# Two small buffers are declared ahead of the weight slots of a two-block transformer kernel

## The reference

```python
# first block:  x = x + fox_mixer(rmsnorm(x));  x = x + nsa_mixer(rmsnorm(x));  x = rmsnorm(x)
# second block: x = x + hgrn2(rmsnorm(x)); x = x + conv_ffn(rmsnorm(x))
#               x = x + mla(rmsnorm(x));   x = x + conv_ffn(rmsnorm(x))
proj = h @ w_in                       # 1024 x 4112 (fox), 1024 x 3632 (nsa), 1024 x 4096 (hgrn2), 1024 x 576 (mla)
y = (attention_or_recurrence(proj) * gate) @ w_out      # 1024 x 1024 in each mixer
u = h @ w_up                          # 1024 x 5632, twice
y = (silu(conv(gate)) * conv(up)) @ w_down              # 2816 x 1024, twice
```

## Time and profile before

| | |
|---|---|
| three runs | 1018.06, 1018.89, 1016.15 us |
| profiled execution | 1013.38 us |
| its span | 1011.6 us |
| granted TensorE clock, mean | 0.994 |
| PE (matmul) busy | 983.1 us, 97% |
| PEld (weight load) busy | 934.2 us, 92% |
| DVE busy | 766.2 us, 76% |
| ACT busy | 549.7 us, 54% |

### The profile page before, as it was taken

The page is one execution under the profiler, slowest core; times in us unless marked ns, Lnnn a source line. Parts: engine busy times, 40 slices in busy tenths (PEclk is TensorE's granted clock), DMA queues, the critical chain, the costliest instruction groups (busy, mean ns, idle before and its releaser), DMA issues. The chain is left out here.

```text
span 1011.6 us, 20271 instructions
## 1 busy us (share of the span) xinstructions
PE 983.1 (97%) x8132; PEld 934.2 (92%) x8132; DVE 766.2 (76%) x1300; ACT 549.7 (54%) x869; POOL 66.7 (7%) x54
## 2 busy tenths in 40 slices
PE   7999999999999999999999999999999999999997
PEld 5999999898788999899999999999997899999997
DVE  5765776867887768498667888888867668878785
ACT  5644555365666656643556554555775565544541
POOL 3100004000000410000030000000001410000000
PEclk9999999999999999999999999999999999999999
DMA  9544345793212556500564767675531456666631
GB/s 283 175 126 132 135 144 148 222 307 97 84 43 85 161 172 194 182 1 1 162 173 142 213 185 207 172 221 149 152 125 43 126 166 193 184 204 170 201 130 42
DMA packets 184141, 153.08 MB, mean 151 GB/s; under 512 B 12477, under 2 KB 176900, under 8 KB 184068
## 3 DMA queue, kind: packets, MB, share of 16 engines
q1 hardware_dynamic: 183858, 152.01, 50.4%
q10 hardware_dynamic: 210, 0.05, 0.0%
HBM read 148.91 MB, written 1.05 MB: 148 GB/s over the span
## 5 line engine op out<-in xcount | busy, mean ns | idle before, releaser
L447 PE MATMUL bank<-h_high,w_high 128*128 128x256 f32 x1312 | 372.6, 284 | 4.6 <-DVE work L1943 1.4
L448 PE MATMUL bank<-h_low,w_high 128*128 128x256 f32 x1312 | 365.5, 279 | 0.0
L449 PE MATMUL bank<-h_high,w_low 128*128 128x256 f32 x1312 | 365.4, 279 | 0.0
L399 ACT ACTIVATE w_high<-ring 128x2048 fp32r<-128x2048 f32 x137 | 261.7, 1913 | 136.2 <-PE bank L449 129.7
L409 DVE TENSOR_TENSOR w_low<-ring,w_high 128x2048 fp32r<-128x2048 f32 x118 | 270.3, 2292 | 27.1 <-ACT w_high L399 26.8
L447 PEld LDWEIGHTS bank<-h_high,w_high 128*128 128x128 f32 x1312 | 248.7, 190 | 6.8 <-issue 5.5
L448 PEld LDWEIGHTS bank<-h_low,w_high 128*128 128x128 f32 x1312 | 247.3, 188 | 0.5 <-issue 0.5
L449 PEld LDWEIGHTS bank<-h_high,w_low 128*128 128x128 f32 x1312 | 247.3, 188 | 0.0
L447 PE MATMUL bank<-ffn_hidden_high,w_high 128*128 (+1 forms) x352 | 98.3, 279 | 2.8 <-DVE ffn_hidden_low L1128 2.8
L448 PE MATMUL bank<-ffn_hidden_low,w_high 128*128 (+1 forms) x352 | 98.1, 279 | 0.0
L449 PE MATMUL bank<-ffn_hidden_high,w_low 128*128 (+1 forms) x352 | 98.1, 279 | 0.0
(11 more groups left out here) (352 smaller groups left out, 1730.7 us busy)
## 6 DMA issues: line engine op xcount, KB each, us to landing
ring<-in_ffn_w_up_dram SPq DMA_DIRECT2D x44, 1024.0 KB, 6.1
ring<-in_ffn_w_down_dram SPq DMA_DIRECT2D x22, 1024.0 KB, 5.0
ring<-in_fox_w_in_dram SPq DMA_DIRECT2D x16, 1024.0 KB, 5.9
ring<-in_hgrn_w_in_dram SPq DMA_DIRECT2D x16, 1024.0 KB, 5.5
ring<-in_nsa_w_in_dram SPq DMA_DIRECT2D x14, 1024.0 KB, 5.5
ring<-in_fox_w_out_dram SPq DMA_DIRECT2D x4, 1024.0 KB, 5.0
ring<-in_nsa_w_out_dram SPq DMA_DIRECT2D x4, 1024.0 KB, 5.0
ring<-in_hgrn_w_out_dram SPq DMA_DIRECT2D x4, 1024.0 KB, 5.0
```

Of the source, the lines that this page charges most:

```text
L399: i = nc.scalar.activation(dst, src, ACT.Copy)
L447: nc.tensor.matmul(o, ah, bh, start=start, stop=False, **kw)
L448: nc.tensor.matmul(o, ah, bl, start=False, stop=False, **kw)
L449: return nc.tensor.matmul(o, al, bh, start=False, stop=stop, **kw)
```

## The change

The buffers `rstd` and `rstd_half`, of two floats per partition, are declared behind `eps` and `scratch` instead of behind the bfloat16 constants. `rstd_inner` stays. Four buffers of 32 bytes now stand between `h_low` and `w_high`. The weight slots, `cst` and the bfloat16 constants move up by 64 bytes; the weight slots stand 128 bytes above the split activations modulo 256 instead of 64. `rstd_inner` and all that is declared behind it keep their addresses. No instruction, wait, DMA or size is added or taken away.

```diff
         eps, scratch = sb("eps", [P, 1]), sb("scratch", [P, 1])
+        rstd, rstd_half = [sb(n, [P, TT]) for n in ("rstd", "rstd_half")]
         w_hi, w_lo = sb("w_high", [P, NSLOT, SLOT], F32R), sb("w_low", [P, NSLOT, SLOT], F32R)
         ring = sb("ring", [P, NSLOT, SLOT])
...
-        rstd, rstd_half, rstd_in = [sb(n, [P, TT]) for n in ("rstd", "rstd_half", "rstd_inner")]
+        rstd_in = sb("rstd_inner", [P, TT])
```

## The result

The changed kernel is slower. Four runs took 1028.74 to 1031.35 us, median 1030.32; four runs of the kernel before took 1016.15 to 1018.89, median 1018.36. The ratio is 1.0144, with a 95% interval of 1.0100 to 1.0188. The profiled execution took 1031.35 us with a span of 1029.6, against 1013.38 and 1011.6 before.

A forecast was written before the change was run, and what follows sets the result against it. PE was taken as the bound. Products at minus 9.0 us, all else at 0, gave 1004.4 us on the profile and 1009.1 on the runs' median; with some extra slow stretches gone, the forecast was 1008, range 997 to 1027.

The forecast's parts named there:

- VectorE's price per tile: VectorE's work on the weight slots: nearly one price at two offsets, hidden behind PE, taken at 0; at most 8 us uncovered.
- loads and constants: Weight loads landing 64 bytes later: 0, ends -3.4 and +3 us; `cst` and the norm buffers: 0, within 1 us.
- The half that I called slow: About half of some 6400 product matmuls run 4.4 ns slower, making about 14 us in the profiled run.
- rival 1: All products: the offset does nothing, the moment a row starts picks the pattern; 1018 us, 1013 to 1021; chance 0.25.
- the product term: Second FFN, by-token products and hgrn2's output lose their locked slow cadence: 9.0 us less, bounds 14 us either way.
- Rival 2: By-feature products: the new distance locks the slow pattern; 1023 on the profile, some 1025 on the median, 1028 worst; chance 0.29.
- by token with `h` is never fast: By-token products with `h`, at minus 64: slow throughout at 117.8 ns, used as evidence that the offset decides.
- the switch of pace at 216.86 us: Where operand roles change, pace goes from 0.11 to 0.12 us without a wait; used as evidence that the offset decides.

The follow-up runs named there:

- e8: The kernel before, unchanged, profiled once more: 1007.19 us.
- e1: Against the kernel before, `h` and the weight slots both moved up 64 bytes, so their distance stays 64 and the other activations' becomes 128: 1014.59 us.
- e2: Against the kernel before, only `h` moved up 64 bytes, to distance 0 from the weight slots; the other activations stay at 64: 1029.44 us.
- e3: Against the kernel before, `eps` and `scratch` declared behind the bfloat16 constants, so the slots stand at distance 0 from all split activations: 1037.64 us.
- e7: Against the kernel before, more small buffers declared ahead of the weight slots, putting them at distance 320 (64 + 256): 1009.84 us.
- e4: Against the kernel before, six small buffers declared ahead of the weight slots, putting them at distance 192 (minus 64): 1024.03 us.
- e16: Against the kernel before, `h_high` and `h_low` cut from one buffer, every product still at 64 or minus 64: median 1017.69 us, ratio 0.9995.

## Why the prediction was wrong

**Right.** PE is the bound, and only its cadence moved: nothing was added, and VectorE's price per tile stayed (2292 and 2293 ns), as did ACT's. For loads and constants, taken at 0, the new profile shows no cost: PE's idle time fell by 1.8 us. The two patterns of 113.4 and 117.8 ns, with 276 and 281 ns, were read rightly, and so was the estimate of what they are worth: e8 found the kernel at 1007 with 76% fast. (The half that I called slow was 46% of the intervals.) The rule of the Trainium skill (SBUF — State Buffer, Who interferes with whom) that PE never waits on anyone, which I weighed beside rival 1, does not hold here, as by it no address could matter: the distance made 113.3 to 120.0 ns of one form of instruction (e1, e2, e3).

**The step that failed** is the product term: "I take the value between: the slow cadence goes where it is locked for long", minus 9.0 us. The measured term is plus 20.7 us in the profiled execution. I supposed that 128, as the farthest point from 0 in a period of 256, would collide least. The period was right (e7), the supposition wrong: the good place is 64, and 128 is as bad as 32 or 96, within 0.4 ns. So the distance from 0 isn't the measure, and by feature the sign matters (64 against 192, e4). Why 64 is the good place, no run shows.

**Rival 2** had the sign and the argument: plus 64 is a good place, and any move is away from it. It priced the change at most at 1028, because I let the cadence be only 113.4 or 117.8. A third pattern at 118.7 adds 0.9 ns to every product, 6260 x 0.9 = 5.6 us more, and that covers the 3.3 us by which 1030.32 lies above the range's end of 1027. The bound "from all slow, 6400 x 4.4/2 = 14 us above the profile" was a bound by the nearest rows, but rows at 64 can't bound a distance that none of them has. The 232 ns for 512 columns at D 0, 116 per 256, was the one row away from 64 on either side. It spoke for a cost there, and I used it only against 0; for 256 columns D 0 turned out at 120 (e3).

**Two readings of rows were too strong.** That by token with `h` is never fast at minus 64 was chance for the most part: e1 had 48% fast, the control e16 46%. And the switch of pace at 216.86 us says little of which distance is better. In the same trace the roles were exchanged at 208.69 us as well, and there the pace went from slow to fast, and at 214.14, where it stayed fast. A change of distance can throw PE from one pattern to another, either way.

## What to carry to other kernels

Where float32r matmuls each load new weights and PE never rests, measure the distance between two starts, not the duration. Two values of it for one form at one granted clock, with no wait between, are a sign of what was found here, and the offset of the stationary above the moving operand modulo 256 bytes is then worth a scan: in this kernel 64 (and its negative now and then) gave 113.3 ns at best, and every other distance tried gave means of 116.8 to 120. Take before-and-after times of such a kernel over many runs, since this one, unchanged, took anything from 1007 to 1020 us.

## What the runs showed of the hardware

- Matmuls of 128 x 256 in float32r, each with its own weight load, start every 113.3, 117.8, 118.7 or 120.0 ns at the same granted clock of 1.00 (2.4 GHz). The distance of the operands decides which of these occur: 120.0 at 0, 118.7 at 128, and 113.3 or 117.8 at 64.
- At distance 64 the first two both last for more than 150 us, and one product in 24 at distance 48 keeps PE in the fast one for most of the run: 1008.64 against 1017.82 us.
- 113.3 ns may still hold a collision. No run had the loads without the products, or less moving data beside them, so the floor is open. The Trainium skill (TensorE: Matmul & The Clock Gate, section Wait — 56ns, not 53.3ns?) has N / 2.4 GHz + 2.5 ns from start to start of back-to-back matmuls of N columns, an estimate of 109.2 ns for 256 columns by that page; no run here shows it.
